# The same feed-forward products on TensorE in other orders

## The chip, the cores and the metric

The kernel runs on one core of a Trainium2 chip. The metric is the device time of one execution in microseconds (us).

## What is computed

Four transformer layers on a sequence of 512 tokens of width 1024, all in float32. Layers 0 and 1 mix three branches (pooling, latent attention, a linear recurrence); the third ("even") layer has retention and windowed attention; the fourth ("odd") has axial attention. Each layer ends with the feed-forward that this change is about:

```python
h = rms_norm(x, g_ffn[l])
x = x + jnp.square(jax.nn.relu(h @ w_ff1[l])) @ w_ff2[l]      # 1024 -> 4096 -> 1024
```

## The kernel before

**Layout.** Activations lie with the features on the 128 partitions and the 512 tokens along the free dimension, so 1024 features are 8 tiles of 128 x 512. A "unit" makes one output tile of 128 features from 8 input tiles: its weights are 8 blocks of 128x128, 512 KB. There are 440 units, in the order in which one stream of weights lies in memory. Units go round a ring of four (RING): unit u has slot u mod 4 of w_raw, w_hi and w_lo, and in the feed-forwards the PSUM tile ps of the same number.

**Three products for one.** Each operand is split into a high part in float32r and a low part, the rest. A block product is three multiplications into one PSUM tile: high weights with high input, high weights with low input, low weights with high input (the helper `products`, lines 693 to 695). A unit is thus 8 x 3 multiplications of 128x128 weights with 512 columns. A multiplication brings its own weight load; the profile shows the loads apart, as PEld.

**Who makes the weights.** SyncE loads w_raw of a unit once GpSimd (POOL) has made the low part of the unit four before it (line 315). ScalarE (ACT) copies w_raw to w_hi (line 341), for unit u + 3 in its step for unit u, once unit u - 1 is done (`unit_done`). GpSimd subtracts: w_lo = w_raw - w_hi (line 329, semaphore `lo_ready`). A unit on TensorE (PE) waits for its own `lo_ready` and for `evacuated` of the unit four before it. Behind the last real unit four surplus ones are loaded and split, and not multiplied.

**Feed-forward** (`ff`). It goes in FF_GROUPS = 4 groups of 1024 hidden features, each 8 up units and 8 down units, so 64 units. After an up unit, VectorE (DVE) takes relu times the norm's factor (line 1126), ScalarE squares it and copies its high part (lines 380 and 382), VectorE makes the low part (line 1119, `ff_ready`). The first unit of each four of a down projection waits for `ff_ready` chunk by chunk. After a down unit VectorE adds the PSUM tile to x (line 1108; in the last group of the first three feed-forwards line 1052, with the next norm's work; in that of the last SyncE stores each tile of x, line 318). The first two units of a feed-forward also hold the token sums of the norm. Layers 0 and 1 are one loop (`pe.Fori(0, DEPTH)`), in which the groups 1 to 3 are a loop too.

Of the kernel before, what the change touches and what calls it, by code (L numbers as in the profile page):

```python
# [15 lines left out]
P = 128  # L16
# [8 lines left out]
S = 512  # L25
D = 1024
KT = D // P
# [38 lines left out]
RING = 4  # L66
# [4 lines left out]
U_FF0 = U_WOUT0 + KT  # L71
FF_GROUPS = 4
# [4 lines left out]
U_EVEN_FF = U_EVEN + EVEN_IN + 16  # L77
U_ODD = U_EVEN_FF + U_FF
ODD_IN = 12
U_ODD_FF = U_ODD + ODD_IN + KT  # L80
N_UNITS = U_ODD_FF + U_FF
N_QUADS = N_UNITS // RING + 1
START = 16
# [37 lines left out]
def build(nc, io):  # L121
    with ExitStack() as ctx:
# [8 lines left out]
        a_hi, a_lo = sb("a_hi", [P, KT, S], F32R), sb("a_lo", [P, KT, S], F32R)  # L131
        b_hi, b_lo = sb("b_hi", [P, KT, S], F32R), sb("b_lo", [P, KT, S], F32R)
        w_raw = sb("w_raw", [P, RING, 8 * P])
        w_hi, w_lo = sb("w_hi", [P, RING, 8 * P], F32R), sb("w_lo", [P, RING, 8 * P], F32R)
# [554 lines left out]
        def _(pe):  # L689
            def products(out, slot, blk, hi, lo, first, last):  # L690

                w_h, w_l = (w[:, slot, blk * P:(blk + 1) * P] for w in (w_hi, w_lo))
                nc.tensor.matmul(out, w_h, hi, start=first, stop=False)  # L693
                nc.tensor.matmul(out, w_h, lo, start=False, stop=False)  # L694
                return nc.tensor.matmul(out, w_l, hi, start=False, stop=last)  # L695

            def unit(u, j, hi, lo, chunk_ready=None, midway=None):

                pe.wait_ge(lo_ready, u + 1)
                pe.wait_ge(evacuated, u - RING + 1 + START)  # L700
                for k in range(KT):
                    if chunk_ready:
                        pe.wait_ge(chunk_ready[0], chunk_ready[1] + k + 1)
                    if midway and k == midway[0]:
                        midway[1]()
                    mm = products(ps[j][:], j, k, hi[:, k, :], lo[:, k, :], k == 0, k == KT - 1)
                mm.then_inc(unit_done, 1)

            def units(u0, quads, hi, lo, chunk_ready=None):

                with pe.Fori(0, quads) as i:
                    for j in range(RING):
                        unit(u0 + i * RING + j, j, hi, lo, chunk_ready if j == 0 else None)

            def turn(bank, src):

# [19 lines left out]
                pe.wait_ge(diag_ready, e + 1)  # L736
                nc.tensor.matmul(ps[bank][:], ones[:], ss[:], start=True, stop=True).then_inc(spread_done, 1)  # L737

            def ff(f, u0, norm_at, n, e, x_in=(a_hi, a_lo), inner=(b_hi, b_lo)):

                def up(g, q):
                    for j in range(RING):
                        unit(u0 + g * 2 * KT + q * RING + j, j, *x_in)

                def down(g):
                    units(u0 + g * 2 * KT + KT, 2, *inner, (ff_ready, (f * FF_GROUPS + g) * KT + 2))

                unit(u0, 0, *x_in, (a_ready, norm_at), (6, lambda: norm_sums(n)))
                unit(u0 + 1, 1, *x_in, midway=(3, lambda: spread(e)))
                unit(u0 + 2, 2, *x_in)  # L750
                unit(u0 + 3, 3, *x_in)
                up(0, 1)
                down(0)
                with pe.Fori(1, FF_GROUPS) as g:
                    with pe.Fori(0, 2) as q:
                        up(g, q)
                    down(g)
# [67 lines left out]
            with pe.Fori(0, DEPTH) as l:  # L825
# [84 lines left out]
                                          k == chunks[0], k == chunks[-1])  # L910
                    mm.then_inc(unit_done, 1)
                units(u + U_WOUT0, 2, c_hi, c_lo, (m_ready, KT * l))
                ff(l, u + U_FF0, 2 * KT * l + KT, 2 * l + 1, 4 * l + 3)


            u = U_EVEN
# [95 lines left out]
            pe.wait_ge(g_ready, KT)  # L1012
            attend(swa, 0, u + EVEN_IN)
            units(u + EVEN_IN + KT, 2, a_hi, a_lo, (swa.o_ready, 0))
            ff(2, U_EVEN_FF, 5 * KT, 6, 16, (b_hi, b_lo), (a_hi, a_lo))


            u = U_ODD
# [2 lines left out]
            k_q_v(u, 2, 10, 18, oq_sq, oq_used, v_raw, (b_hi, b_lo))  # L1021
            attend(axial, 0)
            units(u + ODD_IN, 2, a_hi, a_lo, (axial.o_ready, 0))
            ff(3, U_ODD_FF, 7 * KT, 8, 20, (b_hi, b_lo), (a_hi, a_lo))


        @block.vector
# [777 lines left out]
```

## Time and profile before

| what | value |
|---|---|
| median of 3 runs | 2865.59 us (2864.74 to 2868.92) |
| profiled execution, span from first to last instruction | 2863.3 us |
| TensorE busy | 2766.7 us, 97% |
| VectorE, ScalarE, GpSimd busy | 1072.2, 1068.3, 1066.6 us, 37% each |
| mean granted TensorE clock | 0.988 of 2.4 GHz |
| read from memory | 239.67 MB |

The time of a run is that of the device; the span of the profiled execution leaves out what lies before the first and behind the last instruction. Of the profiled execution only the span is known. "Busy" of TensorE overlaps: multiplications are pipelined and a record is longer than the distance to the next one, so the distance of the starts, not the recorded length, is what a multiplication costs.

### The profile page before, as it was taken

To read this page: it belongs to the slowest core of one execution; us is meant where nothing else is said; L and a number is where in the kernel's file an instruction comes from. 1 tells how busy PE (TensorE), PEld (TensorE's weight loads), DVE (VectorE), ACT (ScalarE), POOL (GpSimd) and SP (SyncE) were. 2 spreads that over 40 slices of the span, in tenths; PEclk is the share of its full clock that TensorE was granted. 3 is DMA by queue.
4 is the path that set the end of the run, shared out by engine and by line. 5 is a ranking of instruction groups with operands and counts; after the bars stand their busy time and mean duration, and the time that the engine had idled before them with its cause. 6 is when DMAs were issued, how large, how long until landed. Compare 5 with 4: busy or idle time off the path is not lost.

```text
span 2863.3 us, 39616 instructions
## 1 busy us (share of the span) xinstructions
PE 2766.7 (97%) x12556; PEld 2236.1 (78%) x12556; DVE 1072.2 (37%) x2021; ACT 1068.3 (37%) x1565; POOL 1066.6 (37%) x448
## 2 busy tenths in 40 slices
PE   6999999999999999999999999899999989999999
PEld 4778878888766888888887668688888876888887
DVE  7653241211467223311137352753111376521111
ACT  5454432333346434332242222443322424533222
POOL 3314444444431344444443224134444431244444
PEclk9999999999999999999999999999999999999999
DMA  3202223222211222222225122112222220122232
GB/s 138 74 23 94 96 88 107 99 95 95 100 60 36 81 95 96 96 93 98 95 95 117 60 71 89 47 59 96 95 95 95 95 81 30 50 94 91 96 101 103
DMA packets 70583, 245.01 MB, mean 86 GB/s; under 512 B 7999, under 2 KB 9407, under 8 KB 70496
## 3 DMA queue, kind: packets, MB, share of 16 engines
q1 hardware_dynamic: 66176, 237.01, 24.8%
q10 hardware_dynamic: 4320, 6.89, 1.1%
q8 instruction: 49, 0.80, 0.1%
q14 instruction: 38, 0.31, 0.0%
HBM read 239.67 MB, written 4.19 MB: 85 GB/s over the span
## 4 chain that ended last, share of the span: by engine, by line
PE 88%; DVE 4%; DVEq 3%; issue 2%; ACT 1%; PEld 1%; DMA 0%; PEldq 0%; ACTq 0%; POOL 0%; SPq 0%; POOLq 0%
PE ps L693 26%; PE ps L694 26%; PE ps L695 26%; PE ps L801 3%; DVEq L1031 2%; PE ps L774 2%; PE ps L787 1%; PE ps L725 1%; PE ps L965 1%; PE ps L737 1%; PE ps L956 0%; PEldq L868 0%; PEld ps L693 0%; PEld ps L695 0%; DVE u_conv L1291 0%
## 5 line engine op out<-in xcount | busy, mean ns | idle before, releaser
L329 POOL TENSOR_TENSOR w_lo<-w_raw,w_hi 128x1024 fp32r<-128x1024 f32 x444 | 1066.4, 2402 | 1796.2 <-ACT w_hi L341 1781.7
L693 PE MATMUL ps<-a_hi,w_hi 128*128 128x512 f32 x1984 | 787.2, 397 | 11.3 <-DVE a_lo L1042 10.2
L694 PE MATMUL ps<-a_lo,w_hi 128*128 128x512 f32 x1984 | 776.8, 392 | 0.0
L695 PE MATMUL ps<-a_hi,w_lo 128*128 128x512 f32 x1984 | 776.4, 391 | 0.0
L341 ACT ACTIVATE w_hi<-w_raw 128x1024 fp32r<-128x1024 f32 x444 | 467.6, 1054 | 511.8 <-PE ps L695 484.1
L693 PE MATMUL ps<-b_hi,w_hi 128*128 128x512 f32 x1376 | 545.9, 397 | 9.2 <-DVE x L1184 8.1
L695 PE MATMUL ps<-b_hi,w_lo 128*128 128x512 f32 x1376 | 537.2, 390 | 0.0
L694 PE MATMUL ps<-b_lo,w_hi 128*128 128x512 f32 x1376 | 537.0, 390 | 0.0
L693 PEld LDWEIGHTS ps<-a_hi,w_hi 128*128 128x128 f32 x1984 | 375.6, 189 | 95.7 <-DVE a_lo L1042 10.2
L694 PEld LDWEIGHTS ps<-a_lo,w_hi 128*128 128x128 f32 x1984 | 375.5, 189 | 81.2 <-issue 4.4
L695 PEld LDWEIGHTS ps<-a_hi,w_lo 128*128 128x128 f32 x1984 | 375.3, 189 | 79.2
L693 PEld LDWEIGHTS ps<-b_hi,w_hi 128*128 128x128 f32 x1376 | 259.5, 189 | 66.4 <-DVE x L1184 9.6
L695 PEld LDWEIGHTS ps<-b_hi,w_lo 128*128 128x128 f32 x1376 | 259.2, 188 | 54.6
L694 PEld LDWEIGHTS ps<-b_lo,w_hi 128*128 128x128 f32 x1376 | 259.5, 189 | 53.8 <-issue 1.5
L1126 DVE SCALAR_TENSOR_TENSOR work<-ps,rstd 128x512 f32<-128x512 f32 x128 | 88.6, 692 | 501.9 <-PE ps L695 498.7
L1108 DVE TENSOR_TENSOR x<-x,ps 128x512 f32 x104 | 71.6, 688 | 464.7 <-PE ps L695 464.7
L380 ACT ACTIVATE sq<-work 128x512 f32<-128x512 f32 x128 | 81.2, 634 | 417.9 <-DVE work L1126 417.9
L1101 DVE TENSOR_TENSOR work<-ps,rstd 128x512 f32<-128x512 f32 x66 | 45.7, 692 | 199.5 <-PE ps L695 199.2
L1052 DVE TENSOR_TENSOR x<-x,ps 128x512 f32 x56 | 38.5, 688 | 104.8 <-PE ps L695 104.8
L556 ACT ACTIVATE probs<-work,lp 128x512 f32<-128x512 f32 x48 | 34.9, 726 | 97.2 <-DVE work L1101 97.0
L425 ACT ACTIVATE work<-ps 128x512 f32<-128x512 f32 (+3 forms) x128 | 59.5, 467 | 12.7 <-PE ps L801 12.4
L350 ACT ACTIVATE a_hi<-x,prm x32 | 23.3, 727 | 102.1 <-DVE x L1052 102.1
(255 smaller groups left out, 2282.0 us busy)
## 6 DMA issues: line engine op xcount, KB each, us to landing
w_raw<-in_w SPq DMA_DIRECT2D x444, 512.0 KB, 3.3
x<-in_x SPq DMA_DIRECT2D x4, 512.0 KB, 7.4
bias_rows<-bias_row ACTq DMA_DIRECT2D x1, 2048.0 KB
out_t<-x SPq DMA_DIRECT2D x8, 256.0 KB, 4.3
bias<-bias_rows ACTq DMA_DIRECT2D x1, 1536.0 KB, 7.0
lp<-in_lp ACTq DMA_DIRECT2D x2, 407.5 KB, 3.2
kt_tab<-in_kt_tab ACTq DMA_DIRECT2D x2, 256.0 KB, 3.2
diff<-in_diff ACTq DMA_DIRECT2D x1, 448.0 KB
```

What stands on the lines that cost most here:

```text
L329: nc.gpsimd.tensor_tensor(w_lo[:, j, :], w_raw[:, j, :], w_hi[:, j, :].bitcast(F32), ALU.subtract).then_inc(lo_ready, 1)
L341: nc.scalar.activation(w_hi[:, j, :], w_raw[:, j, :], ACT.Copy).then_inc(hi_ready, 1)
L380: nc.scalar.activation(sq[:, j % 2, :], work[:, j % 2, :], ACT.Square).then_inc(ff_a, 1)
L425: nc.scalar.activation(work[:, w % 2, 0:nb * P], ps[4 + w % 2][:, 0:nb * P], ACT.Copy).then_inc(t.turned_sb, 1)
L693: nc.tensor.matmul(out, w_h, hi, start=first, stop=False)
L694: nc.tensor.matmul(out, w_h, lo, start=False, stop=False)
L695: return nc.tensor.matmul(out, w_l, hi, start=False, stop=last)
L774: mm = nc.tensor.matmul(ps[s % t.banks][:, 0:nb * P], t.q_st[:, hh % 2, i * P:(i + 1) * P], t.k(it, hh)[:, k0 * P:(k0 + nb) * P], start=Tr ...
L801: mm = nc.tensor.matmul(ps[6 + hh % 2][:, i * P:(i + 1) * P], t.v_st[:, k0 + b, c:c + P], work[:, w % 2, b * P:(b + 1) * P], start=b == 0, ...
L1031: return dve.drain()
L1108: nc.vector.tensor_tensor(x[:, i * RING + j, :], x[:, i * RING + j, :], ps[j][:], ALU.add).then_inc(evacuated, 1)
L1126: nc.vector.scalar_tensor_tensor(work[:, j % 2, :], ps[j][:], 0.0, rstd[:], ALU.max, ALU.mult).then_inc(evacuated, 1)
```

## The change

All 64-unit feed-forwards keep their first four units. The rest is multiplied in another order on TensorE; the products, the inputs and the other engines' programs are the same.

- Layers 0 and 1 (`halves`): each multiplication of 512 columns becomes two of 256. The first 256 columns get their three products, then the other 256, so each weight block is loaded twice as often.
- Even layer (`moving_first`): high-high, then low weights with high input, then high weights with low input.
- Odd layer (`pair`): two output tiles advance together. Each of the three products is made for tile j and at once for tile j + 1, into two PSUM tiles. A pair waits for both tiles' weights and both PSUM tiles, and both tiles are done within its last two multiplications.

```diff
@@ -694,7 +694,7 @@
                 nc.tensor.matmul(out, w_h, lo, start=False, stop=False)
                 return nc.tensor.matmul(out, w_l, hi, start=False, stop=last)
 
-            def unit(u, j, hi, lo, chunk_ready=None, midway=None):
+            def unit(u, j, hi, lo, chunk_ready=None, midway=None, by=None):
 
                 pe.wait_ge(lo_ready, u + 1)
                 pe.wait_ge(evacuated, u - RING + 1 + START)
@@ -703,14 +703,14 @@
                         pe.wait_ge(chunk_ready[0], chunk_ready[1] + k + 1)
                     if midway and k == midway[0]:
                         midway[1]()
-                    mm = products(ps[j][:], j, k, hi[:, k, :], lo[:, k, :], k == 0, k == KT - 1)
+                    mm = (by or products)(ps[j][:], j, k, hi[:, k, :], lo[:, k, :], k == 0, k == KT - 1)
                 mm.then_inc(unit_done, 1)
 
-            def units(u0, quads, hi, lo, chunk_ready=None):
+            def units(u0, quads, hi, lo, chunk_ready=None, by=None):
 
                 with pe.Fori(0, quads) as i:
                     for j in range(RING):
-                        unit(u0 + i * RING + j, j, hi, lo, chunk_ready if j == 0 else None)
+                        unit(u0 + i * RING + j, j, hi, lo, chunk_ready if j == 0 else None, by=by)
 
             def turn(bank, src):
 
@@ -736,14 +736,56 @@
                 pe.wait_ge(diag_ready, e + 1)
                 nc.tensor.matmul(ps[bank][:], ones[:], ss[:], start=True, stop=True).then_inc(spread_done, 1)
 
-            def ff(f, u0, norm_at, n, e, x_in=(a_hi, a_lo), inner=(b_hi, b_lo)):
+            def halves(out, slot, blk, hi, lo, first, last):
+
+                w_h, w_l = (w[:, slot, blk * P:(blk + 1) * P] for w in (w_hi, w_lo))
+                for c in range(2):
+                    at = slice(c * S // 2, (c + 1) * S // 2)
+                    nc.tensor.matmul(out[:, at], w_h, hi[:, at], start=first and c == 0, stop=False, skip_group_check=True)
+                    nc.tensor.matmul(out[:, at], w_h, lo[:, at], start=False, stop=False, skip_group_check=True)
+                    mm = nc.tensor.matmul(out[:, at], w_l, hi[:, at], start=False, stop=last, skip_group_check=True)
+                return mm
+
+            def moving_first(out, slot, blk, hi, lo, first, last):
+
+                w_h, w_l = (w[:, slot, blk * P:(blk + 1) * P] for w in (w_hi, w_lo))
+                nc.tensor.matmul(out, w_h, hi, start=first, stop=False)
+                nc.tensor.matmul(out, w_l, hi, start=False, stop=False)
+                return nc.tensor.matmul(out, w_h, lo, start=False, stop=last)
+
+            def pair(u, j, hi, lo, chunk_ready=None):
+
+                pe.wait_ge(lo_ready, u + 2)
+                pe.wait_ge(evacuated, u - RING + 2 + START)
+                for k in range(KT):
+                    if chunk_ready:
+                        pe.wait_ge(chunk_ready[0], chunk_ready[1] + k + 1)
+                    first, last = k == 0, k == KT - 1
+                    for w, x_in, at in ((w_hi, hi, 0), (w_hi, lo, 1), (w_lo, hi, 2)):
+                        for b in (j, j + 1):
+                            mm = nc.tensor.matmul(ps[b][:], w[:, b, k * P:(k + 1) * P], x_in[:, k, :],
+                                                  start=first and at == 0, stop=last and at == 2)
+                            if last and at == 2:
+                                mm.then_inc(unit_done, 1)
+
+            def ff(f, u0, norm_at, n, e, x_in=(a_hi, a_lo), inner=(b_hi, b_lo), form=None):
 
                 def up(g, q):
+                    if form == "pairs":
+                        pair(u0 + g * 2 * KT + q * RING, 0, *x_in)
+                        pair(u0 + g * 2 * KT + q * RING + 2, 2, *x_in)
+                        return
                     for j in range(RING):
-                        unit(u0 + g * 2 * KT + q * RING + j, j, *x_in)
+                        unit(u0 + g * 2 * KT + q * RING + j, j, *x_in, by=form or products)
 
                 def down(g):
-                    units(u0 + g * 2 * KT + KT, 2, *inner, (ff_ready, (f * FF_GROUPS + g) * KT + 2))
+                    ready = (ff_ready, (f * FF_GROUPS + g) * KT + 2)
+                    if form == "pairs":
+                        with pe.Fori(0, 2) as i:
+                            pair(u0 + g * 2 * KT + KT + i * RING, 0, *inner, ready)
+                            pair(u0 + g * 2 * KT + KT + i * RING + 2, 2, *inner)
+                        return
+                    units(u0 + g * 2 * KT + KT, 2, *inner, ready, by=form or products)
 
                 unit(u0, 0, *x_in, (a_ready, norm_at), (6, lambda: norm_sums(n)))
                 unit(u0 + 1, 1, *x_in, midway=(3, lambda: spread(e)))
@@ -910,7 +952,7 @@
                                           k == chunks[0], k == chunks[-1])
                     mm.then_inc(unit_done, 1)
                 units(u + U_WOUT0, 2, c_hi, c_lo, (m_ready, KT * l))
-                ff(l, u + U_FF0, 2 * KT * l + KT, 2 * l + 1, 4 * l + 3)
+                ff(l, u + U_FF0, 2 * KT * l + KT, 2 * l + 1, 4 * l + 3, form=halves)
 
 
             u = U_EVEN
@@ -1012,7 +1054,7 @@
             pe.wait_ge(g_ready, KT)
             attend(swa, 0, u + EVEN_IN)
             units(u + EVEN_IN + KT, 2, a_hi, a_lo, (swa.o_ready, 0))
-            ff(2, U_EVEN_FF, 5 * KT, 6, 16, (b_hi, b_lo), (a_hi, a_lo))
+            ff(2, U_EVEN_FF, 5 * KT, 6, 16, (b_hi, b_lo), (a_hi, a_lo), moving_first)
 
 
             u = U_ODD
@@ -1021,7 +1063,7 @@
             k_q_v(u, 2, 10, 18, oq_sq, oq_used, v_raw, (b_hi, b_lo))
             attend(axial, 0)
             units(u + ODD_IN, 2, a_hi, a_lo, (axial.o_ready, 0))
-            ff(3, U_ODD_FF, 7 * KT, 8, 20, (b_hi, b_lo), (a_hi, a_lo))
+            ff(3, U_ODD_FF, 7 * KT, 8, 20, (b_hi, b_lo), (a_hi, a_lo), "pairs")
 
 
         @block.vector
```

## Rows read from the trace of the kernel before

**Rows 1.** Page: busy us (share of the span) x instructions, all engines.

```profile
PE 2766.7 (97%) x12556; PEld 2236.1 (78%) x12556; DVE 1072.2 (37%) x2021; ACT 1068.3 (37%) x1565; POOL 1066.6 (37%) x448
```

**Rows 2.** Page: shares of the chain that ended last, by line.

```profile
PE ps L693 26%; PE ps L694 26%; PE ps L695 26%; PE ps L801 3%; DVEq L1031 2%; PE ps L774 2%; PE ps L787 1%; PE ps L725 1%; PE ps L965 1%; PE ps L737 1%; PE ps L956 0%; PEldq L868 0%; PEld ps L693 0%; PEld ps L695 0%; DVE u_conv L1291 0%
```

**Rows 3.** Windows in the feed-forwards: busy PE, PEld, DVE, ACT, POOL; clock, DMA.

```profile
440.00:761.00 321.00, 321.00 (x1418) 265.81 (x1417) 68.70 (x102) 103.55 (x129) 141.08 (x60) 1.00 0.29 97
1187.00:1508.00 321.00, 321.00 (x1418) 265.78 (x1417) 68.70 (x102) 103.52 (x129) 141.08 (x60) 1.00 0.29 97
1972.00:2298.00 326.00, 326.00 (x1440) 269.95 (x1439) 70.59 (x105) 105.62 (x132) 143.31 (x60) 1.00 0.29 97
2537.00:2860.00 323.00, 322.38 (x1423) 266.61 (x1421) 58.57 (x88) 96.03 (x116) 143.14 (x60) 1.00 0.30 98
```

**Rows 4.** Timeline of DVE in a down projection: start us, us.

```profile
1209.78 0.69 DVE L1108 TENSOR_TENSOR x<-x,ps 128x512 f32 x1 [2.48 <-PE ps L695]
...
1236.98 0.69 DVE L1108 TENSOR_TENSOR x<-x,ps 128x512 f32 x1 [4.75 <-PE ps L695]
```

**Rows 5.** Timeline of PE and its weight loads, settled.

```profile
999.91 0.39 PE L693 MATMUL ps<-b_hi,w_hi 128*128 128x512 f32 x1
999.92 0.19 PEld L694 LDWEIGHTS ps<-b_lo,w_hi 128*128 128x128 f32 x1
1000.14 0.39 PE L694 MATMUL ps<-b_lo,w_hi 128*128 128x512 f32 x1
```

**Rows 6.** Window (columns as in rows 3) and timeline of PE after idling.

```profile
36.00:41.00 5.00, 4.15 (x8) 2.63 (x9) 2.32 (x9) 0.00 (x0) 0.00 (x0) 0.50 0.38 127
39.15 0.63 PE L694 MATMUL ps<-a_lo,w_hi 128*128 128x512 f32 x1
...
41.28 0.63 PE L693 MATMUL ps<-a_hi,w_hi 128*128 128x512 f32 x1
```

**Rows 7.** Weight loads: timeline of a float32 product; group of line 693.

```profile
152.84 0.97 PEld L801 LDWEIGHTS ps<-work,v_st 128*128 128x128 f32 x8
L693 PEld LDWEIGHTS ps<-a_hi,w_hi 128*128 128x128 f32 x1984 | 375.6, 189 | 95.7 <-DVE a_lo L1042 10.2 <-issue 8.0
```

**Rows 8.** Timeline of weight loads, float32, 512 columns.

```profile
1617.31 0.19 PEld L965 LDWEIGHTS ps<-work,v_ret 128*128 128x128 f32 x1 [0.24 <-issue]
...
1618.60 0.19 PEld L956 LDWEIGHTS ps<-heads_e 128*128 128x128 f32 x1 [0.24 <-issue]
```

**Rows 9.** Timeline of PE just after another kind of product.

```profile
938.89 0.40 PE L694 MATMUL ps<-a_lo,w_hi 128*128 128x512 f32 x1
...
940.98 0.39 PE L694 MATMUL ps<-a_lo,w_hi 128*128 128x512 f32 x1
```

**Rows 10.** Timeline of PE where the layer loop returns.

```profile
761.34 0.39 PE L695 MATMUL ps<-b_hi,w_lo 128*128 128x512 f32 x1
762.58 0.49 PE L693 MATMUL ps<-a_hi,w_hi 128*128 128x512 f32 x1 [0.85 <-DVE x L1052]
```

**Rows 11.** Timeline of DVE, ACT and POOL in an up projection.

```profile
2603.92 0.69 DVE L1126 SCALAR_TENSOR_TENSOR work<-ps,rstd 128x512 f32<-128x512 f32 x1 [4.82 <-PE ps L695]
...
2606.19 1.04 ACT L341 ACTIVATE w_hi<-w_raw 128x1024 fp32r<-128x1024 f32 x1
...
2607.46 2.39 POOL L329 TENSOR_TENSOR w_lo<-w_raw,w_hi 128x1024 fp32r<-128x1024 f32 x1 [5.56 <-ACT w_hi L341]
```

**Rows 12.** The end: timeline; POOL in the chain; page (median us to landing).

```profile
2858.99 0.39 PE L695 MATMUL ps<-a_hi,w_lo 128*128 128x512 f32 x1
2859.54 0.69 DVE L1108 TENSOR_TENSOR x<-x,ps 128x512 f32 x1 [4.62 <-PE ps L695]
2860.70 2.33 POOL w_lo L329
out_t<-x SPq DMA_DIRECT2D x8, 256.0 KB, 4.3
```

## The prediction

> **What bounds the kernel now.** I read the page first. TensorE (PE) is busy 97% of the span [rows 1], and 78% of the chain that ended last is the three lines of the helper that multiplies [rows 2]. Busy time overlaps on this engine, so I then cut the four feed-forwards out by time. Each stretch is busy from end to end (321.00 of 321.00 us, and 322.38 of 323.00 in the one that reaches the end), at a granted clock of 1.00, which is 2.4 GHz, while VectorE (DVE) is busy about a fifth and ScalarE (ACT) about a third of it [rows 3]. There is no wait of PE left in them: what one pass (one load of 128x128 weights and one stream of 512 columns) takes is what they take.
>
> The length of a pass comes from what hangs on it. In a down projection VectorE takes one tile at the end of each unit, and its starts stand 27.20 us apart over five units [rows 4]: 5.44 us for a unit of 24 passes, 226.7 ns a pass. The timeline shows the same, and that the load of the next weights begins 0.01 us after a stream began and is over (189 ns recorded) before the next stream starts [rows 5, 7]. So loads are hidden.
>
> 512 columns at 2.4 GHz are 213.3 ns; 13.3 ns of each pass are something else. Where the granted clock was 0.50 (1.2 GHz), five passes take 2.13 us, 426 ns each, which is 512/1.2 and nothing more [rows 6]. So the 13.3 ns appear only at full speed. What they hang on, the columns or the pass, decides this change.
>
> **Part by part. Order of the three products (feed-forward of the even layer).** Same passes, same loads, only high-high, low-high, high-low now. Today a pass whose weights equal those before it (line 694 after 693) starts 0.23 us after it, which is also the mean of all [rows 4, 5], and there are as many loads as multiplications [rows 1], so no load is saved or added. Cost 0.
>
> **Two output tiles in turn (feed-forward of the odd layer).** Of 64 units the first four stay; 30 pairs follow. Passes and loads are as many as before, 0 on PE. The waits move: a pair wants both tiles' weights, and frees both slots only at its end. In the up half the step from one unit's end to the next low weights is: VectorE starts at 2603.92, ScalarE's split at 2606.19, GpSimd's (POOL's) ends at 2607.46 + 2.39 = 2609.85, so 5.9 us [rows 11]; the second slot's follows one GpSimd operation later, 8.3 us after the pair's end. Wanted are they one pair later, 48 x 0.2267 = 10.9 us. Slack 2.6 us. In the down half ScalarE and GpSimd have only the splits to do: more slack. The last two inner tiles are wanted after six and seven eighths of the first down pair, 8.2 and 9.5 us after the pair that made them ended; two of VectorE's and four of ScalarE's operations of 0.6 to 0.7 us and one split of 1.04 lie ahead of the last, about 5 us. No wait. If that cover were gone, a miss of 1 us would come 14 times, once for each pair of the up halves, 14 us.
> The end is different. Today the last pass begins at 2858.99, one addition follows at 2859.54, its store takes 4.3 us at the median, so the result is out near 2864.5; a surplus GpSimd split ends at 2863.03 [rows 12]. Now two additions follow (+0.69) and two surplus splits (+2.33, to 2865.4). Both ways the end moves by 0.7 to 0.9 us, a little more if the two stores share; I take +1.0, bounds 0 and +2.3.
>
> **256-column passes (feed-forwards of the first two layers).** Of 64 units the first four stay: 2 x 60 x 24 = 2880 passes of 512 columns become 5760 of 256, with 2880 more loads. A stream now is 106.7 ns at 2.4 GHz, no longer than a load. The before trace has no such pass, so I bound it.
> From below: the 128-column passes of the plain float32 product, with their loads, take 0.97 us for eight, so (0.97 - 0.19)/7 = 111 ns each [rows 7]. A stream of 128 columns is short, so I read it as the rate of loads. Two make 222.9, 3.8 under 226.7: 2880 x -3.8 = -10.9 us.
> From above: if the 13.3 ns belong to the pass whatever its length, 120.0 ns, two 240.0: 2880 x 13.3 = +38.4 us.
> Between: if they belong to the columns, but for the 3 ns that a float32 pass of the same 512 columns shows over 426.7 (three in 1.29 us, 430 each [rows 8]), a pass is (226.7 - 3)/2 + 3 = 114.8 ns, two 229.7: +8.5 us. There is a disturbed form of it too. After a change from another kind of product the first passes are longer, though nothing waits: after the one shown nine take 2.09 us, 232.2 ns each [rows 9]; halved in the same way 117.6 ns, two 235.2: +24.5 us. So the extra time is no constant of the pass: 13.3 ns settled, 18.9 there, and a plain fixed cost wouldn't move. I lean to the columns, and take 115.5 ns, between 114.8 and 117.6 and nearer the settled one, since the settled form fills these stretches: two 231.0, 4.3 x 2880 = **+12.4 us**.
> The Trainium skill ("TensorE: Matmul & The Clock Gate", Back-to-back issue gap) gives N/2.4 + 2.5 ns at full clock, so 215.8 for 512 columns and 109.2 for 256. By its difference the sum would be 2880 x 2.5, an estimate of +7 us; the trace agrees on the size of the fixed part in float32 (3 ns) and disagrees on this kernel's passes (226.7, not 215.8).
> The code of these two feed-forwards doubles. Where PE goes back to the head of the layer loop today, the next multiplication starts 1.24 us after the last instead of 0.23, and 0.85 of it is put down to VectorE [rows 10]. Four returns of the group loop at no more than that are 0 to +4 us; I take 0.
> PSUM tiles are filled in two halves and released at the same point, so VectorE, ScalarE and the weights' ring see only a unit that is some 0.1 us longer: 0.
>
> **Sum.** 0 + 1.0 + 12.4 = +13.4 us on a span of 2863.3. The median of the runs is 2865.59, 2.3 us above the span (what lies around it, the last store above all); the same difference on it gives 2879.
>
> **Rivals.**
> A, *the extra time halves exactly*: passes settle at 113.3 ns, two equal the one they replace. For it: the settled pass is very stable, 5.44 us unit after unit [rows 4]. Against it: the fixed 3 ns. Only the +1.0 of the end is left: 2867.
> B, *faster*: streams hide behind loads. If a short stream gets by without most of the extra time, the load sets the pace at 111.4 ns. Place: the 5760 short passes; price -10.9; it decides from the point where a short pass is under 113.3 ns. For it: the float32 passes of 128 columns do run at that pace. Against it: there the columns come at half the rate, and those columns show no extra time at any length. With the end, 2856.
> C, *fixed cost*: 120.0 ns, +38.4: 2905. For it: the settled pass alone can't tell the two. Against it: rows 9.
> D, *the load no longer hides*: today a load has 226.7 ns to itself, then as many as it takes. In full this would be 106.7 + 111.4 = 218 ns a pass, 2880 x (436 - 227) = +603 us, 3470; each 10 ns of it is 58 us. For it: the trace shows no stream at one column a cycle of this length. Against it: float32 passes of 128 columns, where stream and load are equally long, hide it.
> The Trainium skill (the same page, "What overlaps and what doesn't") says that loads overlap running matmuls only in other row groups. That is rival D in full. The trace disagrees for the passes it has: full 128x128 loads run under full streams [rows 5].
>
> **How the numbers follow.** Forecast (114 to 118 ns) 45%; A 20%; B 10%; C 19%; D, more than 121 ns or code that is late, 6%. 0.2% of 2865.6 is 5.7 us, about what a measurement of this kernel can tell from no change. Faster is B, 0.10; same is A and the lowest edge of the forecast, 0.23; slower the rest, 0.67. The range reaches from B to C, 2856 to 2906, and leaves D and the tails of B and C out, some 0.15.
>
> **What would show it.** The stretch of either early feed-forward (60 units) should be 60 x 24 x 4.3 ns = 6.2 us longer, with 256-column loads and streams 115 to 116 ns apart and still no idle PE; units of the even layer stay 5.44 us; units of the odd layer end in twos, 10.88 us apart, with no wait on GpSimd's low weights; two additions and two splits stand behind the last pass. It would be wrong if short passes stood at 111 or 120 ns, if PE waited for low weights in the odd layer, or if the returns of the group loop showed gaps.

## The result and the profile after

The changed kernel takes 2907.55 us (median of 4 runs, 2902.82 to 2912.72) against 2865.16 us (median of 4, 2863.56 to 2868.92): a ratio of 1.0152, 95% interval [1.0133, 1.0171], 38 to 49 us more. Forecast was 2879 us; the range ended at 2906. The upper two of the four runs had a mean granted clock of 0.986 and 0.987, the others 0.991, so the profiled one (2903.28 us, span 2901.5) is one of the lower two: 38.2 us of span above the kernel before.

The page's first rows, busy time and chain by line, answer to [rows 1, 2]:

```profile
PE 2798.2 (96%) x15436; PEld 2382.5 (82%) x15436; DVE 1077.8 (37%) x2021; ACT 1062.6 (37%) x1565; POOL 1069.1 (37%) x448
PE ps L766 11%; PE ps L693 10%; PE ps L695 10%; PE ps L694 10%; PE ps L746 8%; PE ps L745 8%; PE ps L744 8%; PE ps L753 4%; PE ps L752 4%; PE ps L754 4%; DVEq L1073 3%; PE ps L843 2%; PE ps L816 2%; PE ps L829 1%; PE ps L1007 1%
```

2880 more multiplications and as many more loads, and the other engines as before. The windows of the four feed-forwards (columns as in [rows 3]):

```profile
440.00:781.00 341.00, 340.05 (x2834) 339.85 (x2833) 69.38 (x103) 103.21 (x129) 142.09 (x60) 1.00 0.28 91
1207.00:1547.00 340.00, 340.00 (x2823) 339.47 (x2822) 69.44 (x103) 103.05 (x129) 141.73 (x59) 1.00 0.29 91
2010.00:2336.00 326.00, 326.00 (x1444) 270.00 (x1443) 70.83 (x107) 105.66 (x133) 143.05 (x60) 1.00 0.30 98
2575.00:2901.00 326.00, 320.50 (x1414) 265.04 (x1413) 64.13 (x88) 92.96 (x116) 145.38 (x61) 1.00 0.30 98
```

PE is busy from end to end in the second and third, in the first until the feed-forward ends at 780.05, and in the last until 2895.5. So nothing waits inside them, at a granted clock of 1.00: again the time of a pass is the time of the stretch. In the first two, 340 us hold some 2830 passes, 120 ns each. One line's view (count, duration min/median/max in ns, first and last start) gives it to a tenth of a nanosecond. Here are the high-high passes of each form, from the first down projection on; lines 752 and 766 are those of the even and the odd layer:

```profile
L744 PE MATMUL ps<-b_hi,w_hi x512: 283/283/283, 457.3 to 779.5; 128*128 128x256 f32 x171
L744 PE MATMUL ps<-b_hi,w_hi x512: 283/283/283, 1221.3 to 1543.5; 128*128 128x256 f32 x171
L752 PE MATMUL ps<-a_hi,w_hi x256: 389/389/389, 2025.7 to 2329.6; 128*128 128x512 f32 x128
L766 PE MATMUL ps<-a_hi,w_hi x256: 389/389/389, 2590.7 to 2894.2; 128*128 128x512 f32 x128
```

From the first of these passes to the last lie 56 units of 48 passes, less the last three: 2685 steps in 322.2 us, **120.0 ns**. Of line 752 they are 56 x 24 - 3 = 1341 steps in 303.9 us, 226.6 ns, and of line 766, behind whose last such pass four more follow, 1339 in 303.5, 226.7. So the long passes stayed as they were and two short ones take 240.0 ns instead of 226.7. The settled stretch shows it step by step (timeline of PE, and one of its loads; to be held against [rows 5]):

```profile
1239.79 0.28 PE L745 MATMUL ps<-b_lo,w_hi 128*128 128x256 f32 x1
1239.91 0.28 PE L746 MATMUL ps<-b_hi,w_lo 128*128 128x256 f32 x1
1239.91 0.19 PEld L744 LDWEIGHTS ps<-b_hi,w_hi 128*128 128x128 f32 x1
...
1241.23 0.28 PE L745 MATMUL ps<-b_lo,w_hi 128*128 128x256 f32 x1
```

Twelve steps in 1.44 us. The load's record is as long as before (0.19) and now longer than the distance between two passes: records of loads overlap each other. 1440 long passes became 2880 short ones in each layer: 2 x 1440 x 13.3 ns = **38.4 us**. The end (timeline; ACT, loads and queues left out; answering to [rows 12]):

```profile
2894.89 0.61 PE L766 MATMUL ps<-a_hi,w_lo 128*128 128x512 f32 x2
2895.57 1.29 DVE L1150 TENSOR_TENSOR x<-x,ps 128x512 f32 x2 [9.73 <-PE ps L766]
2896.53 4.64 POOL L329 TENSOR_TENSOR w_lo<-w_raw,w_hi 128x1024 fp32r<-128x1024 f32 x2 [6.06 <-ACT w_hi L341]
```

and the page's row of the stores (median us to landing last):

```profile
out_t<-x SPq DMA_DIRECT2D x8, 256.0 KB, 3.1
```

The store takes 3.1 us at the median (before 4.3). There are two additions and two splits behind the last pair, as forecast. The last pass starts 0.23 us behind 2894.89, at 2895.12, and the span ends 6.4 us later; before, it ended 4.3 us later (2863.3 - 2858.99): **+2.1 us** of span. 38.4 + 2.1 is 2.3 more than the 38.2 of span measured; the mixed stages between the feed-forwards were that much shorter in this execution. Layer 1's alone, from the last pass of layer 0's feed-forward to line 694 behind line 737 in layer 1's, took 404.4 us (before 406.8); in the profiled executions of e1, e12 and e2 below it took 408.5, 403.4 and 403.4, so such a difference needs no other cause. The sum of 40.5 us lies inside the 38 to 49 us of the runs.

One place outside the stretches did change: where PE goes back to the head of the layer loop (timeline of PE, to be held against [rows 10]).

```profile
779.77 0.28 PE L746 MATMUL ps<-b_hi,w_lo 128*128 128x256 f32 x1
782.39 0.49 PE L693 MATMUL ps<-a_hi,w_hi 128*128 128x512 f32 x1 [2.34 <-issue]
```

The next pass starts 2.62 us after the last instead of 1.24, and the wait is put to nothing that the profile shows. With halves alone (e1, e4) it is 2.72 and 2.47, with the feed-forward as before (e3, e12) 1.33 and 1.01. That this comes from the doubled code was not tested, and the 1.4 us are fewer than layer 1's mixed stage scatters by.

### The profile page after: what moved, and what is told of

Same layout as the page of the kernel before. It is cut to its first block, busy times and chain, and to the rows that moved or that the text cites. A ratio compares the mean times of both kernels' runs of the same rounds, so it can differ in the third digit from the quotient of the medians.

```text
span 2901.5 us, 45318 instructions
## 1 busy us (share of the span) xinstructions
PE 2798.2 (96%) x15436; PEld 2382.5 (82%) x15436; DVE 1077.8 (37%) x2021; ACT 1062.6 (37%) x1565; POOL 1069.1 (37%) x448
## 4 chain that ended last, share of the span: by engine, by line
PE 86%; DVE 5%; DVEq 3%; issue 2%; ACT 1%; PEld 1%; PEldq 0%; DMA 0%; ACTq 0%; POOLq 0%; SPq 0%; POOL 0%
PE ps L766 11%; PE ps L693 10%; PE ps L695 10%; PE ps L694 10%; PE ps L746 8%; PE ps L745 8%; PE ps L744 8%; PE ps L753 4%; PE ps L752 4%; PE ps L754 4%; DVEq L1073 3%; PE ps L843 2%; PE ps L816 2%; PE ps L829 1%; PE ps L1007 1%
## 5 line engine op out<-in xcount | busy, mean ns | idle before, releaser
L693 PE MATMUL ps<-a_hi,w_hi 128*128 128x512 f32 x1024 | 414.3, 405 | 12.7 <-DVE a_lo L1084 10.1
L695 PE MATMUL ps<-a_hi,w_lo 128*128 128x512 f32 x1024 | 403.5, 394 | 0.0
L694 PE MATMUL ps<-a_lo,w_hi 128*128 128x512 f32 x1024 | 403.4, 394 | 0.0
L744 PE MATMUL ps<-b_hi,w_hi 128*128 128x256 f32 x1024 | 289.8, 283 | 0.0
L745 PE MATMUL ps<-b_lo,w_hi 128*128 128x256 f32 x1024 | 289.8, 283 | 0.0
L746 PE MATMUL ps<-b_hi,w_lo 128*128 128x256 f32 x1024 | 289.8, 283 | 0.0
L746 PE MATMUL ps<-a_hi,w_lo 128*128 128x256 f32 x896 | 253.6, 283 | 0.0
L745 PE MATMUL ps<-a_lo,w_hi 128*128 128x256 f32 x896 | 253.6, 283 | 0.0
L744 PE MATMUL ps<-a_hi,w_hi 128*128 128x256 f32 x896 | 253.6, 283 | 0.0
L693 PE MATMUL ps<-b_hi,w_hi 128*128 128x512 f32 x416 | 171.8, 413 | 9.7 <-DVE x L1226 8.7
```

The source lines that it names most:

```text
L744: nc.tensor.matmul(out[:, at], w_h, hi[:, at], start=first and c == 0, stop=False, skip_group_check=True)
L745: nc.tensor.matmul(out[:, at], w_h, lo[:, at], start=False, stop=False, skip_group_check=True)
L746: mm = nc.tensor.matmul(out[:, at], w_l, hi[:, at], start=False, stop=last, skip_group_check=True)
```

## The experiments

Two theories stood after the result. **Fixed**: a pass costs columns / 2.4 GHz + 13.3 ns. **Columns**: some 3 ns fixed and the rest in proportion to the columns, as the forecast had it, and the 120.0 ns come from something else about short passes. In the first kernels each part of the change ran by itself.

**e1_halves.** 256-column passes in layers 0 and 1 alone.

```
-ff(2, ..., (a_hi, a_lo), moving_first)
+ff(2, ..., (a_hi, a_lo))
-ff(3, ..., (b_hi, b_lo), "pairs")
+ff(3, ..., (b_hi, b_lo))
```

> Only the 256-column passes of the first two layers; the other two feed-forwards as before. Theory 'fixed' (each pass costs 13.3 ns besides its columns): all of the loss is here, 2880 x 13.3 = +38.4 us, so about 2904 against 2865.5; passes 120.0 ns apart. Rival 'the waits of the pairs share the loss': under +35 us here, the rest in the run with the pairs alone. Rival 'code loading': gaps of PE at the returns of the group loop, more than +40.

2907.16 us (5 runs) against 2865.0 (21 runs), ratio 1.0158 [1.0144, 1.0172]: all of the loss.

```profile
L744 PE MATMUL ps<-b_hi,w_hi x512: 283/283/283, 457.5 to 779.7; 128*128 128x256 f32 x171
```

The same 322.2 us.

**e2_moving_first.** The other order of the three products in the even layer alone.

> Only the other order of the three products in the even layer's feed-forward. Theory: no pass changes, 0 us within the noise (under 1 us), passes 226.7 ns apart. Rival 'equal weights in a row are cheaper to load': the pass of line 694 was the cheap one, and each block product gets longer; at 3 ns per block product it would be 480 x 3 ns = +1.4 us.

2861.36 us (11 runs), ratio 0.9996 [0.9987, 1.0005]; no change. 1341 steps in 304.0 us, 226.7 ns:

```profile
L752 PE MATMUL ps<-a_hi,w_hi x256: 389/389/389, 1984.7 to 2288.7; 128*128 128x512 f32 x128
```

**e3_pairs and e12_pairs_end_single.** Pairs in the odd layer alone, and the same with the last group's down projection unit by unit:

```
+if form == "pairs":
+    g = FF_GROUPS - 1
+    with pe.Fori(0, 2) as q:
+        up(g, q)
+    units(u0 + g * 2 * KT + KT, 2, *inner, (ff_ready, ...))
```

> Only two output tiles in turn in the odd layer's feed-forward. Theory: no wait of PE, passes 226.7 ns apart; only the end is later, by one VectorE addition and one GpSimd split, +0.7 to +2.1 us. Rival 'waits': PE idle before pairs, +5 us or more.

> Pairs in the odd layer alone, as in the run with pairs only, but the down projection of the last group is done unit by unit, so the end of the kernel is that of before. If the two surplus additions and splits behind the last pass are what the pairs cost, their lengthening of the span's tail (about 2 us behind the last pass) goes, and the time is that of before within 0.5 us; one pass costs 226.7 ns in both. If pairs cost anything elsewhere, about +1 us would stay.

Pairs: 2865.26 us (11 runs), ratio 1.0009 [1.0000, 1.0018]. With a single end: 2864.15 us (11 runs) against 2865.16, ratio 1.0000 [0.9991, 1.0009]. The ends of the two (timelines; first the pairs):

```profile
2856.74 0.61 PE L766 MATMUL ps<-a_hi,w_lo 128*128 128x512 f32 x2
2857.42 1.28 DVE L1150 TENSOR_TENSOR x<-x,ps 128x512 f32 x2 [9.73 <-PE ps L766]
```

```profile
2855.05 0.39 PE L695 MATMUL ps<-a_hi,w_lo 128*128 128x512 f32 x1
2855.60 0.69 DVE L1155 TENSOR_TENSOR x<-x,ps 128x512 f32 x1 [4.62 <-PE ps L695]
```

With pairs the last pass starts at 2856.97 and the span ends at 2863.3, 6.3 us later; with a single end 4.35 us later (2859.4), as before. The span's tail is thus the surplus additions and splits, 2.0 us. In the time of the runs it is between 0 and 5 us by the interval, hardly to be told from nothing.

**e4_halves_in_turn.** The two halves of a tile alternate, so each load is of the same weights as the last every second time, and the two passes on one half of the tile are not neighbours. If a short pass waited for its predecessor's result in the same columns, or if equal weights cost less, this would show.

```
+for n, (w_, x_) in enumerate(((w_h, hi), (w_h, lo), (w_l, hi))):
+    for c in range(2):
+        mm = nc.tensor.matmul(out[:, at], w_, x_[:, at], ...)
```

> The 256-column passes alone, but the two halves in turn for each of the three products, so that no pass adds to the columns that the pass before it wrote, and the load of a pass is of the same weights twice. Theory 'fixed': 120.0 ns a pass as before, +38 us. Rival 'the sum in PSUM': passes wait for the same 256 columns to be written by the pass before, which now falls away: under 115 ns a pass, at or under the time before. Rival 'equal weights': the second of each two is shorter than the first.

2902.79 us (one run), and 2683 steps in 321.9 us, 120.0 ns. Neither the neighbour's result nor equal weights change a pass.

```profile
L745 PE MATMUL ps<-b_hi,w_hi x512: 283/283/283, 459.1 to 781.0; 128*128 128x256 f32 x171
```

**e5_300_212 and e6_384_128.** Unequal cuts of the 512 columns.

```
-for c in range(2):
-    at = slice(c * S // 2, (c + 1) * S // 2)
+for c, at in enumerate((slice(0, 300), slice(300, S))):
```

> As the run with the 256-column passes alone, but cut into 300 and 212 columns. Theory 'fixed': the pass of 300 takes 125.0 + 13.3 = 138.3 ns; that of 212 would be 101.7 and is held by its load, 111 to 112 ns. Rival 'grid' (a pass ends on a multiple of 13.3 ns): 133.3 or 146.7 ns for 300. Rival 'load': a short pass costs load plus 13.3, so 120 ns for that of 212. By the first the time is about 2880 x (138.3 + 111.5 - 226.7) = +67 us over before, by the last +91.

> The same cut into 384 and 128 columns. 'Fixed': 160.0 + 13.3 = 173.3 ns and, held by the load, 111.5 ns; +168 us over before. 'Columns' (the extra time goes with the columns, as the prediction had it): 160.0 + 10.7 = about 171 ns. 'Load': 173.3 and 120 ns, +192 us.

2930.43 and 3044.43 us against 2860.64 (one run each). The same view:

```profile
L743 PE MATMUL ps<-b_hi,w_hi x512: 260/286/312, 459.9 to 794.1; 128*128 128x300 f32 x86, 128*128 128x212 f32 x85
```

```profile
L743 PE MATMUL ps<-b_hi,w_hi x512: 221/306/395, 464.9 to 851.3; 128*128 128x384 f32 x86, 128*128 128x128 f32 x85
```

2685 steps in 334.2 us are 248.9 ns for a 300 and a 212 together; fixed says 138.3 + 111 (the rate of loads, which bounds 101.7 here), 249. 386.4 us are 287.8 ns for a 384 and a 128; fixed says 173.3 + 111 = 284. Both are within 4 ns of fixed with a floor of 111 ns under it, but a mixture doesn't give each size by itself. The 384 and 128 lost 184 us, between the 168 that the expectation had for fixed and the 192 for a short pass that costs its load plus 13.3 ns; e15 decides between the two.

**e10_sizes.** One size per feed-forward; the other columns are left out, so the output is not the model's.

```
+at = slice(0, 384)        # 320 in the even layer, 300 in the odd
+nc.tensor.matmul(out[:, at], w_h, hi[:, at], start=first, stop=False)
...
```

> Leaves out the last columns of the products of the feed-forwards: each pass of layers 0 and 1 has 384 columns, of the even layer 320, of the odd layer 300 (the first four units stay at 512), one size by itself, without short passes in between. Fixed theory (columns / 2.4 GHz + 13.3 ns): passes 173.3, 146.7 and 138.3 ns apart, so a unit of 24 passes takes 4.16, 3.52 and 3.32 us. Columns theory (3 ns fixed, the other 10.3 in proportion to the columns): 170.8, 142.8 and 134.0 ns, units of 4.10, 3.43 and 3.22 us. If load and stream merely alternate at their own cost the passes of 300 would not fall below 111 ns either way, so this tells nothing of that.

The 384 in one row (1341 steps in 232.4 us, **173.3 ns**), the 320 and the 300 from timelines inside a unit (20 steps in 2.94 us, **147.0**; 21 in 2.90 us, **138.1**), because their units waited for VectorE at times:

```profile
L743 PE MATMUL ps<-b_hi,w_hi x256: 334/334/334, 452.0 to 684.4; 128*128 128x384 f32 x128
```

```profile
1989.94 0.31 PE L751 MATMUL ps<-b_hi,w_hi 128*128 128x320 f32 x1
...
1992.88 0.31 PE L753 MATMUL ps<-b_hi,w_lo 128*128 128x320 f32 x1
...
2399.97 0.30 PE L759 MATMUL ps<-a_hi,w_hi 128*128 128x300 f32 x1
...
2402.87 0.30 PE L759 MATMUL ps<-a_hi,w_hi 128*128 128x300 f32 x1
```

Fixed expects 173.3, 146.7 and 138.3; columns 170.8, 142.8 and 134.0. With 512 (226.7) and 256 (120.0) five sizes lie on one line to 0.3 ns. The 300 also rule out the grid of e5's expectation, passes that end on multiples of 13.3 ns, which the other four sizes would fit: it wants 133.3 or 146.7. This settles the term that the prediction got wrong.

**e11_all_halves.** Every 512-column product of the kernel in two passes.

> Every unit with full 512-column products, the projections of all layers and the first four units of each feed-forward too, in passes of 256 columns. Fixed theory: +13.3 ns for each pass of 512 that becomes two: the two later feed-forwards change as the first two did, +19.2 us each, and the projections of the mixed stages at the same rate. Counting 24 passes for each unit of 512 columns outside the feed-forwards' 60, that is 5.44 to 5.76 us a unit, +0.32 us. Where a stage is held up by other engines part of it is hidden, so the whole kernel should be at least 76 us longer than before, about 2940 to 3000. Columns theory: 5.44 to 5.54 us a unit and a kernel about 20 to 40 us longer than before. After a stall the extra time is some 19 ns a pass instead of 13.3 in passes of 512 columns; if that too belongs to the pass, the first halves after a stall should stand about 125 ns apart (106.7 + 19), if to the columns about 116.

2984.45 us (one run; before 2865.16), **+119.3 us**. The page counts 22252 multiplications, 9696 more than before:

```profile
PE 2887.8 (97%) x22252; PEld 2744.4 (92%) x22252; DVE 1065.9 (36%) x2021; ACT 1065.1 (36%) x1565; POOL 1068.5 (36%) x448
```

```profile
85.25 0.28 PE L745 MATMUL ps<-a_lo,w_hi 128*128 128x256 f32 x1
...
86.20 0.28 PE L744 MATMUL ps<-a_hi,w_hi 128*128 128x256 f32 x1
```

9696 x 13.3 = 129 us, of which 119 arrived. Some 0.6 us of the rest are passes at a granted clock of 0.50: between 39.27 and 41.83 us of this run twelve steps of 256 columns take 2.56 us, 213 ns each, so two take what one of 512 takes there (426 [rows 6]), and the cut costs nothing; 87 steps are of this kind. What hides the other 9 us in the mixed stages was not traced. The timeline shows passes just after a stall: 8 steps in 0.95 us, 119 ns. The expectation had 125 or 116, so neither theory holds for them: they are no longer than settled passes of 256, while those of 512 were (232.2 against 226.7 [rows 9]). What the first passes behind a stall or another kind of product show is thus no guide to the settled 13.3 ns.

**What the 13.3 ns belong to.** The last six kernels change what a pass reads; their outputs are not the model's.

**e7_64_weights** leaves out the lower 64 output features (half the weight columns):

```
+w_h, w_l = (w[:, slot, blk * P:blk * P + 64] for w in (w_hi, w_lo))
+nc.tensor.matmul(out[0:64, :], w_h, hi, start=first, stop=False)
```

> The same two feed-forwards in passes of 512 columns, but with 64 of the 128 weight columns: the lower 64 features of each output tile are left out there. 'Fixed': 226.7 ns a pass, no change of the time. Rival 'the weights' (the extra 13.3 ns are a quarter cycle for each of 128 weight columns, that is: putting loaded weights to use): half of it falls away, 220.0 ns a pass, 2880 x -6.7 = -19 us.

**e8_bf16** reads the upper two bytes of each 4-byte word of weights and columns (every second bfloat16):

```
+w_h, w_l = (w[...].bitcast(BF16)[:, 1::2] for w in (w_hi, w_lo))
+hi, lo = (x_[:].bitcast(BF16)[:, 1::2] for x_ in (hi, lo))
```

> The same two feed-forwards in passes of 512 columns that read only the upper two bytes of each value, as bf16, at the same distance of four bytes; the results are less exact there. 'The extra time belongs to reading 4-byte values at full rate': some 216 ns a pass, 2880 x -11 = -31 us. 'It belongs to every pass at full clock': 226.7 ns, no change.

**e9_types**, **e13_spacing**, **e14_words** and **e15_short** put constants (tiles wb of 128 and xb of 512 bfloat16) or other places of the data in, a form for each feed-forward:

```
+nc.tensor.matmul(out, wb[:], xb[:], ...)                 # e9, layers 0, 1
+nc.tensor.matmul(out[:, at], wb[:], xb[:, 0::2], ...)    # e9, even
+nc.tensor.matmul(out[:, at], wb[:], xb[:, at], ...)      # e9, odd
+w_h, w_l = (w[:, slot, 0:2 * P:2] for w in (w_hi, w_lo)) # e14, layers 0, 1
+hi, lo = (x_[:, 0::2] for x_ in (hi, lo))                # e14, even
```

> Other data than the kernel's in the passes of the feed-forwards (constants in bfloat16, so the output is not that of the model): layers 0 and 1 512 columns of bfloat16 side by side, the even layer 256 columns taken at every second bfloat16, the odd layer 256 columns side by side. If the 13.3 ns are the pass's own, of whatever type and spacing: 226.7, 120.0 and 120.0 ns apart, units of 5.44, 5.76 and 5.76 us. If they stem from reading 4-byte words, they are less where the columns lie side by side: passes near 213.3 and 106.7 ns, units of 5.12 us. The products here all have the same weights, so a difference from that would show too.

> Replaces the data of the feed-forwards' passes, all of 512 columns: in layers 0 and 1 the weights are the upper halves of the kernel's 4-byte weights (every second bfloat16) and the columns constant bfloat16 side by side; in the even layer the weights are constant bfloat16 side by side and the columns every second bfloat16; in the odd layer both lie side by side and the three passes have three different weight tiles. Passes with both spaced took 225.8 ns, with both side by side and one weight tile 215.8. If the extra time comes with reading the weights 4 bytes apart: about 226, 216 and 216 ns. If with reading the columns 4 bytes apart: 216, 226, 216. If it comes with a change of the weights: 226, 216, 226. If each spaced operand adds a part: both of the first two between 216 and 226.

> float32r with other places of the data, so the output is not that of the model: in layers 0 and 1 the weights are every second column of the ring (8 bytes apart) under 512 columns; in the even layer 256 columns that lie 8 bytes apart, with 128 weight columns side by side; in the odd layer 32 weight columns under 512 columns. If the 13.3 ns come from the weights' bytes or spacing, layers 0 and 1 are longer (up to 240 ns) and the odd layer is shorter (nearer 216). If from the columns' spacing, the even layer's passes are longer than the 120.0 ns of 256 columns side by side, up to 133. If the 13.3 ns are those of a float32r pass whatever its reads, 226.7, 120.0 and 226.7 to 230 ns.

> Layers 0 and 1: the bfloat16 passes of e8 (weights and columns every second bfloat16, the upper halves of the kernel's own words) in 256 columns instead of 512. If the extra 12.5 ns are the pass's own, about 119 ns apart; if for bfloat16 they go with the columns, as the 113.4 ns of constant weights over 256 spaced columns suggest, about 113. Even layer: 192 float32r columns, odd layer: 128 (the other columns of the products are left out). Fixed theory: 80 + 13.3 = 93.3 and 53.3 + 13.3 = 66.7 ns, if nothing else limits. If loads set a floor, as the float32 passes of 128 columns suggest, both stand about 109 to 111 ns apart, and no cut of 512 columns into more than four can be paid with less than that. Units may here wait for weights; the spacing inside a unit is what counts.

First e7 (view of line 742) and e8 (timeline of VectorE: its additions stand six units apart, in layer 0 and then in layer 1):

```profile
L742 PE MATMUL ps<-b_hi,w_hi x256: 389/393/398, 456.9 to 765.3; 128*64 128x512 f32 x128
L742 PEld LDWEIGHTS ps<-b_hi,w_hi x256: 133/134/135, 456.6 to 765.1; 128*64 128x64 f32 x128
```

```profile
463.87 0.69 DVE L1158 TENSOR_TENSOR x<-x,ps 128x512 f32 x1 [2.45 <-PE ps L745]
...
496.27 0.69 DVE L1158 TENSOR_TENSOR x<-x,ps 128x512 f32 x1 [4.71 <-PE ps L745]
...
1214.12 0.69 DVE L1158 TENSOR_TENSOR x<-x,ps 128x512 f32 x1 [4.76 <-PE ps L745]
...
1246.75 0.69 DVE L1158 TENSOR_TENSOR x<-x,ps 128x512 f32 x1 [4.75 <-PE ps L745]
```

Then e9, the views of its lines 745 and 762, and of the even layer additions six units apart (timeline of VectorE):

```profile
L745 PE MATMUL ps<-xb,wb x480: 379/379/390, 436.5 to 746.7; 128*128 128x512 bf16 x160
L762 PE MATMUL ps<-xb,wb x960: 272/273/283, 2506.8 to 2820.8; 128*128 128x256 bf16 x192
```

```profile
2061.60 0.69 DVE L1179 TENSOR_TENSOR x<-x,ps 128x512 f32 x1 [4.76 <-PE ps L755]
...
2094.24 0.69 DVE L1179 TENSOR_TENSOR x<-x,ps 128x512 f32 x1 [4.75 <-PE ps L755]
```

The views of the three lines of e13, of e14, and of one of e15:

```profile
L746 PE MATMUL ps<-xb,w_hi x480: 379/379/391, 437.4 to 747.6; 128*128 128x512 bf16 x160
L753 PE MATMUL ps<-a_hi,wb x256: 386/387/388, 1960.6 to 2263.4; 128*128 128x512 bf16 x128
L759 PE MATMUL ps<-xb x480: 379/379/390, 2503.3 to 2813.4; 128*128 128x512 bf16 x160
```

```profile
L746 PE MATMUL ps<-b_hi,w_hi x256: 394/394/394, 457.1 to 770.0; 128*128 128x512 f32 x128
L754 PE MATMUL ps<-a_hi,w_hi x256: 405/409/417, 2005.7 to 2314.1; 128*128 128x256 f32 x128
L761 PE MATMUL ps<-a_hi,w_hi x256: 391/394/397, 2576.8 to 2887.5; 128*32 128x512 f32 x128
```

```profile
L749 PE MATMUL ps<-b_hi,w_hi x512: 274/274/274, 461.8 to 766.1; 128*128 128x256 bf16 x171
```

And of e15 the timeline of PE in the even layer, and a window (columns as in [rows 3]) in the odd one:

```profile
2000.80 0.27 PE L759 MATMUL ps<-a_lo,w_hi 128*128 128x192 f32 x1
...
2002.47 0.27 PE L759 MATMUL ps<-a_lo,w_hi 128*128 128x192 f32 x1
```

```profile
2500.00:2600.00 100.00, 100.00 (x471) 100.00 (x471) 19.00 (x28) 30.49 (x36) 47.00 (x21) 0.50 0.32 105
```

A pass is the stretch over its steps. A row that begins with the inner tiles spans 56 units (1341 steps, or 2685 for halves), one that begins with the first of the 60 units 1437 (or 2877). The extra is the pass less columns / 2.4 GHz. The granted clock was 1.00 in all these stretches.

| run, form | pass, ns | extra, ns |
|---|---|---|
| before: float32r, 512 columns | 226.7 | 13.3 |
| after: float32r, 256 | 120.0 | 13.3 |
| e7: float32r, 512, 64 weight columns | 308.4 / 1341 = 230.0 | 16.7 |
| e14: float32r, 512, 32 weight columns | 310.7 / 1341 = 231.7 | 18.4 |
| e14: float32r, 512, weights 8 bytes apart | 312.9 / 1341 = 233.3 | 20.0 |
| e14: float32r, 256 columns 8 bytes apart | 308.4 / 1341 = 230.0 | 123.3 |
| e8: bfloat16, 512, weights and columns 4 bytes apart | 32.40 / (6 x 24) = 225.0, and 32.63 / 144 = 226.6 | 11.7, 13.3 |
| e15: the same, 256 | 304.3 / 2685 = 113.3 | 6.7 |
| e13: bfloat16, 512, only the columns 4 bytes apart | 302.8 / 1341 = 225.8 | 12.5 |
| e9: the same, 256 | 32.64 / (6 x 48) = 113.3 | 6.7 |
| e13: bfloat16, 512, only the weights 4 bytes apart | 310.2 / 1437 = 215.9 | 2.5 |
| e13: bfloat16 side by side, 512, three weight tiles | 310.1 / 1437 = 215.8 | 2.5 |
| e9: bfloat16 side by side, 512, one weight tile | 310.2 / 1437 = 215.9 | 2.5 |
| e9: the same, 256 | 314.0 / 2877 = 109.1 | 2.5 |

The extra time does not follow the length of the load: fewer weights shorten the load's record (134 ns instead of 188) and not the pass, and bfloat16 passes don't mind weights 4 bytes apart or a change of weights. That loads have no part in it is not shown for float32r, since there fewer or spaced weights lengthen the pass, by 3.3 to 6.6 ns. In bfloat16 the reading of the columns is what matters: side by side all but 2.5 ns go away, 4 bytes apart 10 ns come back. In float32r only the wider spacing was tried: columns 8 bytes apart stream at half the rate (256 of them take as long as 512). But in float32r the extra is the same at every length, and in bfloat16 with spaced columns it halves with them (12.5 and 6.7), which is rival A's rule. So the 13.3 ns are shown to be a fixed part of each float32r pass, and where in the pass they arise stays open.

192 float32r columns take 111 ns in e15 (15 steps in 1.67 us), not 93.3: loads set that floor, as the expectation's last sentences had it. The same holds for 128 columns. The first units of the odd layer's stretch run at a granted clock of 1.00 (timeline of PE):

```profile
2404.99 0.28 PE L766 MATMUL ps<-b_hi,w_hi 128*128 128x128 f32 x1
...
2415.03 0.28 PE L766 MATMUL ps<-a_hi,w_hi 128*128 128x128 f32 x1
```

90 steps in 10.04 us, 111.6 ns, not 66.7, so below 256 columns a pass with its load no longer follows the columns. A pass that costs its load plus 13.3 ns would take more than that, so this rival is out. At 2415.9 PE then sat idle for 2.2 us, waiting for VectorE, and from 2419 to the end of the stage the granted clock was 0.50, which is 1.2 GHz. There passes of 128 columns start 213 ns apart (471 of them touch the 100 us of the row above), twice the 106.7 that 128 columns take at 1.2 GHz: the floor is there too.

## Why the prediction was wrong

Its failed step is the costing of the 256-column pass. The trace gave one settled length, 226.7 ns at 512 columns, and that 13.3 ns of it were no streaming. The prediction gave these to the columns ("I lean to the columns", 115.5 ns, +12.4 us); measured are 120.0 ns and +38.4 us. This was rival C word for word, "120.0 ns, +38.4: 2905", with a chance of 19%.

What was held against C was [rows 9]: 18.9 ns behind another kind of product, so "the extra time is no constant of the pass". That a quantity differs in two states of the engine doesn't say what it scales with in either of them. e11 shows how little the one tells of the other: just behind a stall a pass of 256 takes 119 ns, near the 117.6 that the prediction worked out for it, and then 120.0. The halved value was about right for the first passes behind a stall and wrong for the 2880 of each stretch. No row of the trace before could tell C from the forecast; a settled pass of another length didn't exist in it. Then the ends of the range should have carried more weight, and the range should have reached past C's sum: 2865.6 + 38.4 + 2.3, with the end at its own upper bound, is already 2906.3, and the three runs before spread over 4 us.

- *Order of the three products, 0*: right. 226.7 ns, ratio 0.9996 (e2).
- *Pairs, 0 on PE*: right. Line 766 at 226.7 ns, PE busy until its last pass.
- *End, +1.0 us, bounds 0 to +2.3*: +2.1 of span in the profiled executions (after and e3), gone in e12, which is inside the bounds at their upper part; the surplus splits weigh as the prediction reckoned the worst case, since the span ends with them. In the runs' times pairs cost 1.0009 [1.0000, 1.0018].
- *Lower bound of a short pass, 111 ns from loads*: the rate is real as a floor. Passes of 192 and of 128 columns stand at 111 and 111.6 (e15), and the cuts 300 + 212 and 384 + 128 fit it within 4 ns. Passes of 256 float32r columns don't reach it (B is out); bfloat16 ones side by side go below it, to 109.1.
- *Rival A, 113.3 ns*: not for float32r, exactly so for bfloat16 with spaced columns.
- *Rival D, loads no longer hide*: out; its other half, code that is late, at most as under the returns below. The Trainium skill ("TensorE: Matmul & The Clock Gate", What overlaps and what doesn't) would have full-size loads wait for running multiplications; at 120.0 ns a pass with a load in each they don't.
- *Back-to-back gap of the same page of the Trainium skill*, N/2.4 + 2.5 ns: the trace agrees for bfloat16 side by side, to 0.1 ns (215.8 and 109.1), and disagrees for this kernel's float32r (226.7 and 120.0).
- *Returns of the group loop, 0*: right. The 322.2 us over four groups leave no gap beside 2685 equal steps. The return of the layer loop, whose row the prediction used only as a bound for them, is the one that grew, from 1.24 to 2.62 us; the sum had no term for it.
- *From span to time, +2.3 us*: this took the median of the runs less the span of another execution. In each run on record the time is 1.8 us above its own span. It moves the forecast by 0.5 us at most.

## What to carry to other kernels

Where TensorE is bound by its passes, count the passes: in float32r, at a granted clock of 1.00 and 256 to 512 columns, each cost columns / 2.4 GHz plus 13.3 ns, with about 111 ns as the least where every pass loads its weights, so cutting a stream in two is 13.3 ns lost for each cut, and the order of passes with as many loads is worth nothing. When the trace has one size only, a fixed part and a proportional part can't be told apart in it: let the forecast's range cover both, and don't read the settled rate from passes just behind a stall. A change that groups outputs in pairs was free on the way here and pays at the very end, where nothing follows to hide the second of a pair.

## What was not expected of the hardware

- bfloat16 columns side by side cost 215.8 ns a pass of 512, the same columns 4 bytes apart 225.8; float32r columns 8 bytes apart run at half the rate (230.0 ns for 256).
- Half or a quarter of the weight columns makes a float32r pass longer, not shorter: 230.0 and 231.7 ns against 226.7.
- Passes of 192 and of 128 float32r columns with a load in each take the same 111 to 112 ns at a granted clock of 1.00; at 0.50 those of 128 take 213 ns, as long as 256 columns.
- At a granted clock of 0.50 the fixed part is gone: 213 ns for 256 columns (e11), 426 for 512 [rows 6].
- In e15 the granted clock fell from 1.00 to 0.50 some 1 us after PE had sat idle for 2.2 us in a stretch of 128-column passes 111.6 ns apart, and stayed there for the rest of the stage, although the records show PE busy throughout.
